# Two layer normalizations of a tuned block: squares gathered during the out projection, gating on ScalarE

## What is computed

```python
u = h * (1.0 + scale[:, None, :]) + shift[:, None, :]
y, yc = mixer(u, uc, ...)                      # windowed attention, then neighbourhood attention
h = layer_norm(DEEPNORM_ALPHA * h + gate[:, None, :] * y, ln_g[i], ln_b[i])
if ctx_out:
    hc = layer_norm(DEEPNORM_ALPHA * hc + gate_c * yc, ln_g[i], ln_b[i])

def layer_norm(x, g, b):
    mu = jnp.mean(x, axis=-1, keepdims=True)
    var = jnp.mean(jnp.square(x - mu), axis=-1, keepdims=True)
    return (x - mu) * lax.rsqrt(var + LN_EPS) * g + b
```

## Time and profile before

| | us |
|---|---|
| median of three runs | 3232.0 (3227.84 to 3232.37) |
| the profiled execution's own time | 3234.13 |
| its span, first to last instruction | 3232.3 |
| TensorE busy | 3111.7 (96%) |
| VectorE busy | 2000.9 (62%) |
| ScalarE busy | 1301.4 (40%) |
| GpSimd busy | 759.0 (23%) |
| TensorE's granted clock, mean | 0.987 of full |

### The profile page before, as it was taken

One profiled execution on the slowest core, in us unless ns is written; L12 is line 12 of the kernel. 1 busy time (PEld: TensorE's weight loads), 2 busy tenths in 40 slices (PEclk: granted clock), 3 DMA queues, 4 the chain that ended last, 5 costly groups with the idle time before them and its releaser, 6 DMA issues.

```text
span 3232.3 us, 47842 instructions
## 1 busy us (share of the span) xinstructions
PE 3111.7 (96%) x18134; PEld 2580.3 (80%) x18134; DVE 2000.9 (62%) x3834; ACT 1301.4 (40%) x2340; POOL 759.0 (23%) x324
## 2 busy tenths in 40 slices
PE   9999999999999989999899999999899999999987
PEld 6888888777777767877799889888677777777765
DVE  5676677555656657965855555556755555555555
ACT  5534443444444440022444444440344444454412
POOL 3223332222222214443211121114112121211221
PEclk9999999999999999999999999999999999999998
DMA  3111111111111137621200010043101111110241
GB/s 118 46 40 46 46 59 46 60 59 53 53 53 61 64 145 297 214 78 52 92 30 31 31 43 31 34 194 148 77 27 51 45 51 45 46 37 33 73 164 68
DMA packets 64828, 237.79 MB, mean 74 GB/s; under 512 B 7008, under 2 KB 10080, under 8 KB 63600
## 3 DMA queue, kind: packets, MB, share of 16 engines
q1 hardware_dynamic: 31680, 115.91, 10.4%
q10 hardware_dynamic: 32944, 119.10, 9.9%
HBM read 185.11 MB, written 49.87 MB: 73 GB/s over the span
## 4 chain that ended last, share of the span: by engine, by line
PE 83%; DVE 9%; ACT 4%; issue 2%; DVEq 1%; DMA 1%; ACTq 0%; SPq 0%; POOL 0%; POOLq 0%
PE ps L1318 22%; PE ps L189 15%; PE ps L360 9%; PE ps L2238 7%; PE ps L1382 5%; PE ps L1348 5%; PE ps L1364 4%; PE ps L891 3%; PE ps L482 3%; PE ps L868 2%; PE ps L133 2%; PE ps L852 1%; DVE fox_l L1469 1%; PE ps L853 1%; DVE wa_l L941 1%
## 5 line engine op out<-in xcount | busy, mean ns | idle before, releaser
L210 POOL TENSOR_TENSOR w_hi<-raw,small 128x1024 fp32r<-128x1024 f32 x160 | 333.9, 2087 | 2388.9 <-PE ps L1318 1085.6
L212 POOL TENSOR_TENSOR w_lo<-raw,w_hi 128x1024 fp32r<-128x1024 f32 x160 | 424.9, 2656 | 22.8
L1318 PE MATMUL ps<-nb_u_hi,w_hi 128*128 128x512 f32 (+1 forms) x640 | 249.5, 390 | 6.4 <-DVE nb_q_lo L2485 4.5
L1318 PE MATMUL ps<-nb_u_lo,w_hi 128*128 128x512 f32 (+1 forms) x640 | 246.4, 385 | 0.0
L1318 PE MATMUL ps<-nb_u_hi,w_lo 128*128 128x512 f32 (+1 forms) x640 | 246.1, 385 | 0.0
L1480 DVE TENSOR_TENSOR nb_pt_lo<-ps,nb_pt_hi 128x512 fp32r<-128x512 f32 x208 | 143.9, 692 | 136.7 <-ACT nb_pt_hi L1407 136.4
L360 PE MATMUL ps<-u_hi,w_hi 128*128 128x512 f32 x528 | 212.9, 403 | 5.9 <-ACT silu_h L539 2.6
L360 PE MATMUL ps<-u_hi,w_lo 128*128 128x512 f32 x528 | 208.6, 395 | 0.0
L1318 PE MATMUL ps<-u_hi,w_hi 128*128 128x512 f32 x512 | 208.4, 407 | 0.0
L1318 PE MATMUL ps<-u_hi,w_lo 128*128 128x512 f32 x512 | 208.2, 407 | 0.0
L360 PE MATMUL ps<-u_lo,w_hi 128*128 128x512 f32 x528 | 208.1, 394 | 0.0
(11 more groups left out here) (357 smaller groups left out, 8035.0 us busy)
## 6 DMA issues: line engine op xcount, KB each, us to landing
raw<-in_w_stream SPq DMA_DIRECT2D x160, 512.0 KB, 3.4
h_sb<-in_w_ada ACTq DMA_DIRECT2D x16, 1024.0 KB, 5.0
nf_b<-nf_rows ACTq DMA_DIRECT2D x16, 512.0 KB, 4.4
nb_bias<-in_rel_bias ACTq DMA_DIRECT2D x16, 448.0 KB, 3.9
y_parts<-wa_y_hi ACTq DMA_DIRECT2D x8, 640.0 KB, 2.9
y_parts<-wa_y_lo ACTq DMA_DIRECT2D x8, 640.0 KB, 4.2
la_out_yh<-y_parts SPq DMA_DIRECT2D x8, 640.0 KB, 10.2
la_out_yl<-y_parts SPq DMA_DIRECT2D x8, 640.0 KB, 11.2
```

What stands on the lines that cost most here:

```text
L210: pool.tensor_tensor(w_hi[:, s, :], raw[:, s, :], zero, ALU.add)
L212: pool.tensor_tensor(w_lo[:, s, :], raw[:, s, :], w_hi[:, s, :].bitcast(F32), ALU.subtract).then_inc(w_ready, 1)
L1318: mm = pe.matmul(ps[:, b:b + ch["n"]], w(slot, k), u[:, k, ch["c0"]:ch["c0"] + ch["n"]], start=k == 0 and p == 0, stop=k == KT - 1 and p == 2)
```

## The change

- Right after turn 2 TensorE takes an early mean for each token, from feature tile 0 alone (one spread matmul per 512 columns, in banks 6 and 7; in the first layer the context part right after turn 1, which ScalarE copies to `c_ctx`). Eight times it is the centre.
- While the projection goes on, VectorE writes each tile's distance from that centre into `t2` (`from_centre`), ScalarE squares it in place (`squares`), and VectorE adds it to `acc2` (`add_square`). At `k` = 4 VectorE also takes the centres with tokens on partitions (`centre_tokens`, 10 or 8 small reductions).
- The gating moves from VectorE to ScalarE (`gate`, with `taken` telling that a bank is free). The order of ScalarE's queue mixes gates, squares and residual loads.
- `meanwhile` moves to before tile 7. After tile 7's pieces TensorE sums `acc` and `acc2` per token (`token_sums`: one column of output per 128 tokens), and spreads the mean of `acc`; VectorE corrects the variance by the square of the distance of mean and centre (three tiny instructions) and subtracts the mean from the tiles: all eight ahead of the modulation in the first layer; in the second three ahead of the scalings, and the other five among them.
- The mask `win` leaves `consts` for a tile of its own, with a load on ScalarE's queue ahead of the first layer's mixer. The stores of the result are issued by SyncE, the stores of `h` after the square root. TensorE's loop over turns is written out.

```diff
-                with pe.Fori(0, KT // 2) as i:
-                    for m in range(2):
...
-                broadcast_means(pe, self.acc, self.cols, 0, True, False)
-                pe.wait_ge(self.added, self.base + KT)
-                broadcast_means(pe, self.h[:, KT - 1, :], self.cols, 0, False, True).then_inc(self.mean_sum, 1)
-                pe.wait_ge(self.gated, 1 + self.base + KT)
                 for k in range(KT):
-                    pe.wait_ge(self.sq_set, self.base + k + 1)
-                    broadcast_means(pe, self.sq[:, k % 2, :], self.cols, 3, k == 0, k == KT - 1
-                                    ).then_inc(self.sq_sum, 1)
+                    m = k % 2
+                    free = [w for b in (range(3) if m == 0 else range(3, 8)) for w in mixer.free(b)]
+                    project(pe, self.n_out + k, m, self.yh, self.yl,
+                            self.span(3 * m, free + self.bank_taken(k - 2)), self.chunk,
+                            ready=ready, tiles_outer=m == 0 and not self.by_parts,
+                            late=last if self.by_parts else None)
+                    if k == 1:
+                        pe.wait_ge(self.added, self.base + 1)
+                        if self.cols == TC:
+                            broadcast_means(pe, self.h[:, 0, T:TC], C, 6, True, True).then_inc(self.early_mean, 1)
+                    if k == 2:
+                        pe.wait_ge(self.early_copied, 1)
+                        broadcast_means(pe, self.h[:, 0, 0:T], T, 6, True, True).then_inc(self.early_mean, 1)
+
+                pe.wait_ge(*self.bank_taken(KT - 2)[0])
+                for p, (t, n) in enumerate(self.chunks):
+                    keep_busy(pe, 2, 4)
+                    pe.wait_ge(self.last_summed, self.parts0 + p + 1)
+                    self.token_sums(pe, self.acc, t, n, 0)
+                    if p == 1:
+                        pe.wait_ge(*self.bank_taken(KT - 1)[0])
+                        broadcast_means(pe, self.acc[:, 0:T], T, 3, True, True).then_inc(self.mean_sum, 1)
+                    if p == 2:
+                        broadcast_means(pe, self.acc[:, T:TC], C, 5, True, True).then_inc(self.mean_sum, 1)
+                    keep_busy(pe, 2, 6 if p else 2)
+                    pe.wait_ge(self.squared, self.parts0 + p + 1)
+                    mm = self.token_sums(pe, self.acc2, t, n, 1)
+                mm.then_inc(self.token_sum, 1)
                 spread_rows(pe, self.cols, self.diag, 0, 3 + self.l, 18)
                 if self.l == 0:
                     keep_busy(pe, 6, 10)
+
...
+                def squares(j, cols=slice(0, self.cols), n=0):
+                    act.wait_ge(self.early_set, self.early0 + j + n + 1)
+                    buf = self.t2[:, j % 2, cols]
+                    nc.scalar.activation(buf, buf, ACT.Square).then_inc(self.early_sq, 1)
+
+                def gate(k, part=0):
+                    whole = k < KT - 1
+                    spans = [(0, T)] + self.chunks[2:] if whole else [self.chunks[part]]
+                    last = whole or part == len(self.chunks) - 1
+                    act.wait_ge(self.added, self.base + k)
+                    act.wait_ge(self.chunk, 2 * self.base + (len(self.chunks) - 1) * k
+                                + (len(self.chunks) - 1 if last else part + 1))
+                    if last:
+                        act.wait_ge(w_used, self.n_out + k + 1)
+                    for t, n in spans:
+                        src = ps[:, 3 * (k % 2) * CH + t:3 * (k % 2) * CH + t + n]
+                        g = gates[:, self.l, k, :]
+                        ins = nc.scalar.activation(self.tmp[:, 0, t:t + n], src, ACT.Identity, bias=g[:, 2:3],
+                                                   scale=g[:, 1:2] if t >= T else g[:, 0:1])
+                    ins.then_inc(self.taken, 1)
+
+                gate(0)
+                gate(1)
+                if self.l == 0:
+                    act.wait_ge(self.early_mean, 1)
+                    nc.scalar.copy(self.c_ctx[:], ps[:, 6 * CH:6 * CH + C]).then_inc(self.early_copied, 1)
                 residual(1)
+                gate(2)
+                squares(0)
...
+                squares(6)
+                last = KT - 1
+                gate(last, 0)
+                squares(last, slice(0, CH), 0)
+                gate(last, 1)
+                if self.l == 0:
+                    gate(last, 2)
+                    squares(last, slice(CH, T), 1)
+                    squares(last, slice(T, TC), 2)
+                else:
+                    squares(last, slice(CH, T), 1)
                 load_sqrt_table(act)
                 act.wait_ge(stat_var, 2 + self.l)
                 standard_deviations(act, self.cols, None, small[:, 2:3])
+                if self.l == 0:
+                    for k in range(KT):
+                        act.wait_ge(self.centred, self.base + k + 1)
+                        act.dma_start(h_dram[k, :, 0:T], self.h[:, k, 0:T]).then_inc(b_stored, 16)
...
+                def from_centre(j, cols=slice(0, self.cols)):
+                    dve.drain()
+                    buf = self.t2[:, j % 2, :]
+                    lat = slice(cols.start, min(cols.stop, T))
+                    if lat.stop > lat.start:
+                        ins = dve.scalar_tensor_tensor(buf[:, lat], ps[:, 6 * CH + lat.start:6 * CH + lat.stop], -8.0,
+                                                       self.h[:, j, lat], ALU.mult, ALU.add)
+                    if cols.stop > T:
+                        ins = dve.scalar_tensor_tensor(buf[:, T:TC], self.c_ctx[:], -8.0, self.h[:, j, T:TC],
+                                                       ALU.mult, ALU.add)
+                    ins.then_inc(self.early_set, 1)
+
+                def add_square(j, cols=slice(0, self.cols), n=0):
+                    dve.wait_ge(self.early_sq, self.early0 + j + n + 1)
+                    dve.drain()
+                    return dve.tensor_tensor(self.acc2[:, cols], self.acc2[:, cols], self.t2[:, j % 2, cols], ALU.add)
+
+                def centre_tokens():
+                    dve.drain()
+                    for j in range(self.cols // P):
+                        src = ps[:, 6 * CH + j * P:6 * CH + (j + 1) * P] if j < T // P else \
+                            self.c_ctx[:, j * P - T:(j + 1) * P - T]
+                        dve.tensor_tensor_reduce(self.t2[:, 1, j * P:(j + 1) * P], src, ident, 8.0, small[:, 0:1],
+                                                 ALU.mult, ALU.add, self.c_tok[:, j:j + 1])
...
+                    if k == KT - 1:
+                        add_square(KT - 2)
+                        if meanwhile:
+                            meanwhile(dve)
...
+                        dve.wait_ge(self.taken, self.early0 + k + part + 1)
                         dve.drain()
                         ins = dve.scalar_tensor_tensor(self.h[:, k, cols], self.res[:, m, cols], ALPHA,
                                                        self.tmp[:, 0, cols], ALU.mult, ALU.add)
                         if last:
                             ins.then_inc(self.added, 1)
+                        if k == KT - 1:
+                            dve.drain()
+                            dve.tensor_tensor(self.acc[:, cols], self.acc[:, cols], self.h[:, k, cols], ALU.add
+                                              ).then_inc(self.last_summed, 1)
+                            from_centre(k, cols)
+                            if part == 0:
+                                add_square(k, cols).then_inc(self.squared, 1)
                     if k < KT - 1:
                         dve.drain()
                         dve.tensor_tensor(self.acc[:], self.acc[:], self.h[:, k, :], ALU.add).then_inc(self.summed, 1)
+                    if k == 2:
+                        dve.wait_ge(self.early_mean, 2 + l)
+                        from_centre(0)
+                        add_square(0)
+                    elif k == 3:
+                        from_centre(1)
+                        from_centre(2)
+                        add_square(1)
+                        add_square(2)
+                    elif k == 4:
+                        centre_tokens()
+                        from_centre(3)
+                        from_centre(4)
+                        add_square(3)
+                        add_square(4)
+                    elif k == 5:
+                        from_centre(5)
+                        add_square(5)
+                    elif k == 6:
+                        from_centre(6)
+                for p, (t, n) in list(enumerate(self.chunks))[1:]:
+                    add_square(KT - 1, slice(t, t + n), p).then_inc(self.squared, 1)
+
+                n = self.cols // P
+                dve.wait_ge(self.token_sum, l + 1)
+                dve.tensor_tensor(self.d_tok[:], ps[:, 0:n], self.c_tok[:], ALU.subtract)
                 dve.drain()
-                dve.wait_ge(self.mean_sum, l + 1)
```

(53 more changed lines are left out.)

72 lines of the change are left out of this document (27 added, 45 removed).

## The result

| | before | after |
|---|---|---|
| median, us (7 runs each, interleaved) | 3229.5 (3227.2 to 3232.4) | 3240.2 (3237.7 to 3244.7) |
| profiled execution, own time | 3234.1 | 3242.0 |
| VectorE busy | 2000.9 | 2028.0 |
| TensorE's granted clock, mean | 0.987 | 0.981 |

The ratio is 1.0034, 95% interval 1.0024 to 1.0043: the change costs 8 to 14 us. The forecast of 3240.0, slower, held, but that it was met to 0.2 us is luck: the difference was +10.7 where I forecast +8.0, and the median of before, 3232.0 in three runs, is 3229.5 in seven. Among the parts, too, misses of opposite sign met in the sum.

The account below looks back on a forecast made before the run. TensorE's out projection was taken to bound both layers, with only the work after its last matmul exposed. First layer +9.2 and second -1.2 gave +8.0 us on a median of 3232.0: 3240.0, range 3236 to 3245.

Parts of the forecast that it names:

- VectorE late by the standing: Out projections: VectorE waits for GpSimd's splits, 10.8 and 5.3 us, reaching tile 7 9.9 and 2.1 us late.
- First layer from there: First layer from VectorE's start on tile 7 to the modulation: 6.1 + 9.4 + 4.0 + 10.0 us.
- The variance to the diagonal: First layer's tail after the token sums: variance, first subtraction, reciprocal and diagonal, 4.0 us.
- Seven subtractions: First layer's tail, last step before the modulation: seven subtractions of the mean at 1.42, 10.0 us.
- Second layer from there: Second layer after tile 7 starts: 11.7 to token sums' end, 6.2 filling and spread, 17.6 scalings to last bias addition.
- The clock: Both tails: TensorE idles, its clock halves; mostly hidden in waits for VectorE, 1.3 and 0.9 us let through.
- the clock stays low: Rival, both tails: bursts with gaps don't bring the clock back, some +5 us each, 3250; chance 0.13.
- Early means: Added means in TensorE's unbroken chain during the out projections: +2.4 us first layer, +2.0 second.
- Sum: Whole change: first layer +9.2, second -1.2, together +8.0 us.
- the 0.6 for the next projection's start: First projections after the first layer's tail: 0.6 us let through for TensorE's lowered clock.
- VectorE doesn't stand: Rival: added VectorE operations slip between GpSimd's splits, removing 10.8 and 5.3 us; 3223.7 if the clock holds; chance 0.10.
- Half of it: Rival, no change: splits shift too, half of the 16.1 us of standing is left; 3232, up to 3237; chance 0.27.

Follow-up runs that it names:

- thin_splits: Changed kernel with GpSimd's splits of six weight units per layer cut to 32 of 1024 columns, output not the reference's; 3221.2 us.
- late_splits: Changed kernel with GpSimd waiting for the first layer's last sum of squares before splitting the next mixer's first two units; 3236.5 us.
- clock_held: Changed kernel with 84 (first layer) and 20 (second) filling matmuls for 4 before the first token sums, 10 for 2 before the first sums of squares; 3242.8 us.
- win_moved: Kernel before the change, with only the mask `win` moved out of `consts` into its own tile and load; 3229.4 us.
- win_room: As win_moved, plus an unused tile of 640 columns behind `consts` so every tile keeps its old address; 3230.4 us.
- held_short: Changed kernel with 44 (first layer) and 13 (second) filling matmuls before the first token sums, 7 for 2 before the first sums of squares; 3234.8 us.
- later_held: Changed kernel with tables and centres behind the last sum of squares, 20 filling matmuls before first token sums, 10 before first sums of squares; 3230.8 us.
- rearranged_gap: As rearranged, with 4 filling matmuls in place of 14 ahead of the first layer's first token sums; 3220.9 us.
- rearranged: Changed kernel with two splits held back, two sums of squares and some subtractions reordered, filling matmuls resized; everything computed; 3218.3 us.

## Where the prediction was right and where not

- **VectorE late by the standing: right, and sized right.** 10.8 of standing laid out, 10.6 measured; 9.9 late, 9.4 measured; second layer 5.3 and 5.8 (from the end of turn 4), 2.1 and 1.5 late. thin_splits and late_splits confirm the cause.
- **First layer from there.** 6.1 + 9.4 for the pieces and TensorE's queue: by the 13.4 of clock_held in place of 17.9, measured 15.0 without the clock (14.1 by the estimate above). The variance to the diagonal 4.0: 3.7. Seven subtractions 10.0: 10.0.
- **Second layer from there.** 11.7: 10.8 with the clock held. 6.2 and 17.6: 5.8 and 17.4.
- **The clock: the failed step.** I let 1.3 and 0.9 us through, on the argument that the slow bursts lie in TensorE's waits for VectorE. They don't: once VectorE's pieces are done, TensorE has a backlog, and it drains at half speed. At least 4.5 and 5.4 measured, in place of 1.3 and 0.9. The last rival, "the clock stays low", had the mechanism and the price (some +5 each) nearly right, and I gave it 0.13.
- **Early means** 2.4 and 2.0: 2.15 and 1.72.
- **Sum.** Forecast +9.2 and -1.2, +8.0. From the table: tails +8.0 and -0.9, early means +3.9, together +11.0, against 10.7 between the medians. So the forecast is 2.7 to 3 us short: the clock terms were too small by 3.2 (at least) and 4.5, the others, all small, too large by some 4, and the 0.6 for the next projection's start was not found. That the profiled execution came out at 3242.0 for a forecast of 3242.1 is an accident: the two executions are 7.9 apart because all that comes ahead of the first layer's out projection took 5.2 off the difference, the projection itself 0.5, and the path between the layers put 2.7 on it. And 3240.0 met 3240.2 because the base that I stated, 3232.0, was 2.5 above the median of seven runs, which made up for the 2.7 that the difference lacked.
- **The base of the second layer.** win_moved and win_room, whose second layer is as before, have a tail of 40.2, not 41.9: there the clock didn't fall in the same wait. So of the 41.7 that I set the change against, 1.7 was this execution's own clock, and against 40.2 the change loses 0.8 in that tail.
- **Rivals.** "VectorE doesn't stand" at 3223.7 is what thin_splits measured by taking the standing away: 3221.2. "Half of it" was wrong: the splits didn't slip.

Not settled: the path from the modulation to the end of the second projection took 874.6 to 879.6 us in these ten traces, 874.95 in before and 879.4 in after, without order by kernel. Of after's 2.7 us beyond the early mean, 1.6 are the clock again: it is at 0.62 and 0.53 from 3110 to 3114, as the second projection starts, and the projection's first 123 matmuls take 30.02 us, where late_splits at 1.00 takes 28.44. In before the clock is at 1.00 there too. Whether the change makes such a fall likelier these traces don't say, and a cost of 1 us more can't be told from them.

## What to carry to other kernels

Work moved off the critical engine into another's slack costs more than its own length where the instructions stand for a third engine: list VectorE's instructions with two SBUF inputs, count GpSimd's beside them, and hold back those that nobody wants yet. A tail of short bursts is priced at both levels of TensorE's clock, and fillers are safe only if no gap is left before and between the bursts; after gaps of 1 to 2.5 us the clock fell more often than not here. Together these turned +0.34% into -0.36% here.

## What was not expected of the hardware

- In otherwise equal waits the clock fell or didn't. Idle of 0.73 and 0.63 us close together (first layer of thin_splits), 1.07 (first layer of held_short), 1.45 (later_held) and 2.41 (rearranged_gap) was followed by about 0.50; idle of 0.67 and 0.71 (second layer of rearranged and rearranged_gap) and 1.28 (second layer of held_short) was not; the 2.5 us before the squares in the old second layer was in before and was not in win_moved and win_room. With no idle up to the end of the token sums (clock_held in both layers, thin_splits and later_held in the second, rearranged in the first) it never fell. What decides is open.
- The first block's last projections run at two levels, 0.2288 or 0.2333 us from matmul to matmul, in kernels with the same text and addresses for that stage (after and held_short) and with a granted clock of 1.00 in both: 613 against 602 matmuls in 140 us (after and before). Three of the four slow traces come from one chip, which has a quick one too. What sets the level is open.
